# A transformer block pair on one core: TensorE multiplies ones by ones at the start and around the first modulation fold

## The reference

```python
mod = jax.nn.silu(c) @ w_ada[l] + b_ada[l]
shift1, scale1, gate1, shift2, scale2, gate2 = jnp.split(mod[:, None, :], 6, axis=-1)

h = rms_norm(x, g_norm1[l]) * (1.0 + scale1) + shift1
proj = h @ w_in[l]
na_q, na_k, na_v, q_lat, kv_lat, k_rot, gate_na, gate_mla = jnp.split(proj, split_at, axis=-1)
# rms_norm(x, g) = x * rsqrt(mean(x * x) + EPS) * g
```

## Time and profile before

| | us |
|---|---|
| median of 3 runs | 1112.86 |
| the runs | 1111.52, 1112.86, 1113.27 |
| span of the profiled execution | 1111.0 |
| PE busy | 1066.9 (96%) |
| PEld busy | 738.1 (66%) |
| DVE busy | 385.5 (35%) |
| ACT busy | 275.5 (25%) |
| DMA | 335 MB, mean 302 GB/s |

### The profile page before, as it was taken

The page is one execution under the profiler, slowest core; times in us unless marked ns, Lnnn a source line. Parts: engine busy times, 40 slices in busy tenths (PEclk is TensorE's granted clock), DMA queues, the critical chain, the costliest instruction groups (busy, mean ns, idle before and its releaser), DMA issues.

```text
span 1111.0 us, 17393 instructions
## 1 busy us (share of the span) xinstructions
PE 1066.9 (96%) x7054; PEld 738.1 (66%) x7054; DVE 385.5 (35%) x998; ACT 275.5 (25%) x619; POOL 52.9 (5%) x85
## 2 busy tenths in 40 slices
PE   6999999999999999999999989989999999999998
PEld 4786776688756455465555655546548888887567
DVE  1298966532631212111121122111333011433851
ACT  2124134600511111111111101111322101213851
POOL 0000202013100000000000000001000001100001
PEclk9999999999999999999999999999999999999999
DMA  9999387955579999999999999999997434100201
GB/s 386 340 421 421 125 343 313 419 223 189 216 303 382 420 421 420 420 414 422 418 422 421 420 420 421 385 422 421 418 396 297 140 125 152 39 1 1 114 1 38
DMA packets 48560, 335.22 MB, mean 302 GB/s; under 512 B 5440, under 2 KB 6816, under 8 KB 8672
## 3 DMA queue, kind: packets, MB, share of 16 engines
q1 hardware_dynamic: 46080, 329.01, 72.9%
q10 hardware_dynamic: 2176, 3.37, 1.0%
q0 software_dynamic: 224, 1.70, 0.4%
HBM read 333.02 MB, written 1.05 MB: 301 GB/s over the span
## 4 chain that ended last, share of the span: by engine, by line
PE 85%; DMA 8%; DVE 4%; ACT 1%; issue 1%; SPq 1%; DVEq 0%; ACTq 0%
PE bank L1080 13%; PE bank L538 12%; DMA ring<-experts 8%; PE bank L1124 6%; PE bank L1035 5%; PE bank L1221 5%; PE bank L924 5%; PE bank L945 3%; PE bank L455 3%; PE bank L980 3%; PE bank L1309 3%; PE bank L830 2%; PE bank L1264 2%; PE bank L845 2%; PE bank L668 2%; PE bank L553 2%
## 5 line engine op out<-in xcount | busy, mean ns | idle before, releaser
L1080 PE MATMUL bank<-ring,arena 128*32 128x512 f32 (+1 forms) x1120 | 173.7, 595 | 10.6 <-DMA ring<-experts 10.5
L538 PE MATMUL bank<-hT,ring 128*128 128x256 f32 x608 | 134.4, 381 | 0.7 <-ACT hT L1503 0.7
L538 PEld LDWEIGHTS bank<-hT,ring 128*128 128x128 f32 x608 | 114.5, 190 | 21.7 <-issue 6.6
L1080 PEld LDWEIGHTS bank<-ring,arena 128*32 128x32 f32 (+1 forms) x1120 | 50.7, 120 | 115.0 <-issue 114.7
L1124 PE MATMUL bank<-ring,arena 128*32 128x512 f32 (+1 forms) x560 | 87.5, 596 | 5.2 <-DMA ring<-experts 5.2
L924 PEld LDWEIGHTS bank<-arena 128*128 128x128 bf16 x1152 | 66.2, 98 | 13.3 <-issue 10.6
L924 PE MATMUL bank<-arena 128*128 128x128 bf16 x1152 | 72.3, 219 | 2.0 <-ACT arena L1669 2.0
L2310 DVE TENSOR_TENSOR yhalf<-bank,yhalf 128x512 fp32r<-128x512 f32 x48 | 33.2, 692 | 96.7 <-ACT yhalf L1706 96.7
L1440 POOL TENSOR_TENSOR hT<-hT 128x256 f32<-128x256 f32 x30 | 21.8, 726 | 829.5 <-ACT hT L1497 828.1
L2297 DVE SCALAR_TENSOR_TENSOR arena<-bank,arena 128x256 f32<-128x256 f32 x24 | 11.6, 484 | 133.4 <-ACT arena L1698 122.2
L1124 PEld LDWEIGHTS bank<-ring,arena 128*32 128x32 f32 (+1 forms) x560 | 25.2, 119 | 49.0 <-issue 45.8
(11 more groups left out here) (391 smaller groups left out, 1431.3 us busy)
## 6 DMA issues: line engine op xcount, KB each, us to landing
ring<-experts SPq DMA_DIRECT2D x188, 1024.0 KB, 14.1
ring<-stream SPq DMA_DIRECT2D x119, 1024.0 KB, 12.1
ring<-experts SPq DMA_DIRECT2D x8, 512.0 KB, 7.7
arena<-consts POOLq DMA_DIRECT2D x1, 1408.0 KB, 12.0
resid<-x SPq DMA_DIRECT2D x1, 1024.0 KB, 5.1
resid<-ctx ACTq DMA_DIRECT2D x1, 1024.0 KB, 9.9
arena<-stream SPq DMA_DIRECT2D x1, 1024.0 KB, 9.8
bias_room<-rpb ACTq DMA_DIRECT2D x2, 438.0 KB, 5.5
```

Source lines behind the costliest of these rows:

```text
L538: mm = mmul(o[:, 0:n_tok], w[:, k, t * P:(t + 1) * P], hT[:, k, 0:n_tok], start=(k == 0), stop=(k == KT - 1))
L1080: mm = mmul(o[at:at + n_slots, :], xg[:, kk, at:at + n_slots], w[g][:, k, :], start=(kk == 0), stop=(kk == KT - 1))
```

## The change

A helper `keep_busy(b, n)` is added to PE's program: n matmuls of `ones` (128x128) with itself, into the first 128 columns of PSUM bank b, with no semaphore and with a result that nobody reads (the next group in bank 5 starts with `start=True`). It is called three times, for bank 5: 13 matmuls ahead of the sums of squares, 6 ahead of the first fold and 6 behind it. GpSimd's memset of `ones` becomes its first.

```diff
+            def keep_busy(b, n):
+                for _ in range(n):
+                    mmul(bank[b][:, 0:P], ones[:], ones[:], start=True, stop=True)
+
             pe.wait_ge(S("ones_set"), 1)
+            keep_busy(5, 13)
             rms_sums("sum1", 0, 256, squared="sq1")
             pe.wait_ge(S("silu_c"), 1)
...
             ada_slab("ada1", 0)
             ada_slab("ada1", 4)
             pe.wait_ge(S("fold_in"), 16)
+            keep_busy(5, 6)
             ada_fold(("first", 0))
+            keep_busy(5, 6)
             two_ks(0, 0)
...
             g = nc.gpsimd
+            g.memset(ones[:], 1.0).then_inc(S("ones_set"), 1)
             g.memset(silc[:], 0.0).then_inc(S("silc_zero"), 1)
             g.memset(silc2[:], 0.0).then_inc(S("silc_zero"), 1)
-            g.memset(ones[:], 1.0).then_inc(S("ones_set"), 1)
```

## The result

| | before | changed |
|---|---|---|
| median, us | 1112.74 (12 runs) | 1116.08 (12 runs) |
| lowest and highest | 1110.48, 1114.42 | 1113.43, 1119.85 |
| ratio, 95% interval | | 1.0028 (1.0018 to 1.0039) |
| span of the profiled execution | 1111.0 | 1114.5 (its own time 1116.35) |
| PE instructions added | | 100 (25 matmuls, 4 each) |

The ratio and its interval are those on record; they are not exactly the quotients of the two medians, but differ from them by up to 0.1%. The forecast of 1109.4 us and its range, 1107.4 to 1112.6, were wrong, and the sign with them.

What follows compares the result with a forecast made beforehand. TensorE bounds the kernel (85% of the chain). Terms 3.02 - 0.78 + 0.73 + 1.12 - 0.5 - 0.05 = 3.5 us less, so span 1111.0 - 3.5 = 1107.5, plus 1.86 gives 1109.4 us; range 1107.4 to 1112.6.

Steps and rivals of the forecast that it cites:

- The sums: Sums of squares before the first fold: 16 records at 0.219 us, 3.50 instead of 6.52 us, 3.02 us less.
- The fold's fillers: Six fillers ahead of the first fold: take 1.32 us where it had waited 0.54, a price of 0.78 us.
- The second block hidden: Six fillers behind the first fold: 1.32 to 1.53 us inside a hole of 1.65, costing nothing.
- the slow stretch gone: Clock stays up around 19.3 to 22.7 us: 8 records save 0.73 us, 32 narrow ones save 1.12.
- The rival drawn from the rule in the Trainium skill: Clock rises early but still falls around 19 us: 2.2 us less, no slab waits, 1110.6 us; chance 0.13.
- What is late next: Weight slabs land as before; the sixth, at 20.95, costs a new 0.5 us wait, the ninth 0.05.
- Reaches the end: From the third pair of tiles to program end: the 3.5 us saved is kept whole, span 1107.5 us.
- the argument on the ring: Between 120 and 135 us the DMA ring is full and waits for PE; nothing stays tied to the start.
- The slower rival: Around the first fold, 12 gap fillers at the lower clock add 3.1 to 4.0 us: 1116 to 1117; chance 0.06.
- Rival 4: Gain given back later; a clock fall at 145 us going gives 1107.7, a new one 1111.1; chance against 0.09.

Runs made afterwards that it cites:

- the one that overran the squares: Changed kernel with 25 one-column matmuls (128 columns of weights) ahead of the sums, no gap fillers, 100 more instructions than before: 1121.95 us, ratio 1.0090.

## Why the prediction was wrong

- *The sums* (forecast 3.02 us less): right in mechanism, a little high. Their result was read 2.69 us earlier, since the group took 3.72 us at the upper level instead of the 3.50 reckoned, and began 0.1 later.
- *The fold's fillers* (0.78 us): right. The second block began at 12.40 and pushed the fold to 13.84; of the 2.69 us, 1.98 were left behind it, a price of 0.71.
- *The second block hidden, the slow stretch gone* (0.73 + 1.12): right in this profile. 8 records in 1.97 and 32 in 1.93 us, from 1.98 to 3.62 us ahead. The rival drawn from the rule in the Trainium skill ("TensorE: Matmul & The Clock Gate", the table in "Why this matters for your kernels") did not come true near 19 us in this execution, nor in the one with gap fillers alone. But the runs do not settle that the gap fillers do it: with three wide fillers ahead of the sums and empty gaps (1.67 and 0.49 us) the clock stayed up too, with 13 narrow ones it fell. No rule on the length of a hole follows from these profiles.
- *What is late next: "so they land as before"*: this is the first step that failed. The slabs land 2.5 us apart as the prediction has it, but a packet of PE's own code comes between them, and its place moves with the count of PE's instructions and with PE's pace. The sixth slab came at 22.37 instead of 20.95. The term was 0.5 us and measured 1.42 (from the end of the second fold). The group behind the wait took another 1.84 us (7.10 - 5.26) that no term held; 1.65 of it is the slow clock, since the same group took 5.45 us behind a wait at the upper level. Why the clock fell there stays open. So 3.5 us at the third pair became 0.36. With 20 instructions instead of 100 the slab was on time and the forecast's 3.5 measured 3.33.
- *Reaches the end*: the argument on the ring held, but "I take the 3.5 us as kept whole" left out the second failed step, which no term of the sum and no rival held: what the mere 100 instructions do some 800 us later, at the branch behind the experts (by the traces, through the loading of PE's code). It costs 3.17 us of stall and 1.7 to 1.9 of slow clock, 5.1 in the profile. Alone, it costs 1116.65 - 1113.08 = 3.6 us in the medians (100 against 48 instructions).
- *The slower rival* (gap fillers at the lower level, 1116 to 1117): the number came near the result for a wrong reason; the gap fillers ran at 1.4 to 1.6 us a block, the upper level.
- *Rival 4* (a fall of the clock that goes or comes): the one at 145 to 150 us was there after as before, 0.66 in that window in both. The new fall behind the branch is a part of the second failed step.

The sum of the profile: 0.36 ahead, some 1.2 more gained among the experts, 5.1 lost: 1114.5 against 1111.0. Most of that 1.2 us came between 700 and 740 us, where PE waits for the experts' slabs, and it is a loss in the profile before rather than a gain: there a slab landed 3.97 us behind the last (718.08 behind 714.11), where the changed kernel has 2.5. All nine other profiles gained 0.8 to 1.8 us on it at this place, those with next to no added work too. What held up that slab, and whether it does so in every execution of the kernel before, stays open. That a code piece delays a slab was varied only through the count of instructions, so the order of cause (packet, then slab) is the trace's reading. It is a steady one: slabs land 2.5 us apart, and the one step of 3.7 to 4.0 us among the first eleven comes right behind the packet in every profile. With the packet at 19.2 to 20.3 us it was the sixth slab (22.4 to 22.5), with it between 21.6 and 22.8 the seventh (24.8 to 25.0), at 23.8 the eighth (27.4), and at 27 the ninth (29.8), which is where the kernel before has it.

## What to carry to other kernels

Work added only to keep TensorE's clock up should be put into as few instructions as possible: here the same columns in 32 instead of 100 instructions made the difference between 0.9992 and 1.0028, and a single block of 12 instructions (0.9973, up to 0.9984) was better than the 100 and no worse than the 32. The loss is one of position, though: it was absent up to 52 and there at 100, no other count was run, and in another program a few instructions may be enough. In a long unrolled program ask of every added instruction what it does to the loading of the code behind it, above all at branches that skip a block: look for idle time with the releaser "issue" and for a packet on the instruction queue beside it. And when a stretch is pulled forward, look at what else the DMA moves beside the load whose landing then decides.

## What the runs showed that I had not expected

- Behind a branch over a block PE ran one matmul record and then stood 3.17 and 3.18 us in two kernels with 100 more instructions; a third, the one that overran the squares, stood 3.3 us. None of the profiles with 12 to 52 more had that stall.
- The clock fell behind this stall in all three: in the changed kernel 0.51 over 824.5 to 828.0 us, so that a 3.2 us stall costs about 5.
- The spread between executions of one kernel mostly follows the mean granted clock. Of the changed kernel's 12 runs the three with 0.996 and above had spans of 1111.6 to 1112.5 us, the one with 0.991 had 1118.0. A profile taken once can hold a fall that another execution does not have: in the run with 12 more instructions the clock was low in a stretch around 147 us (0.50 in the window below) for twice as long as in the earlier trace rows.

```profile
140.00:145.00 5.00, 5.00 (x26) 2.98 (x25) 1.37 (x2) 3.46 (x7) 0.00 (x0) 0.89 0.90 349
145.00:150.00 5.00, 5.00 (x10) 2.85 (x9) 2.08 (x7) 2.75 (x3) 0.00 (x0) 0.50 1.01 421
```
